# Where the expert tiles, the weight ring and the normalised rows begin in SBUF: from offsets of 96 and 128 bytes to multiples of 512

## The reference

```python
def expert_choice_moe(h, w_router, w_gate_e, w_up_e, w_down_e):
    b, s, _ = h.shape
    cap = EC_CAPACITY * s // N_EXPERTS            # 2 * 512 // 16 = 64 rows for each of 16 experts
    affinity = jax.nn.softmax((h @ w_router).astype(jnp.float32), axis=-1)
    top_aff, idx = lax.top_k(jnp.swapaxes(affinity, 1, 2), cap)
    ...
    xe = h[bidx, idx]
    hid = jax.nn.silu(jnp.einsum('becd,edf->becf', xe, w_gate_e)) * jnp.einsum('becd,edf->becf', xe, w_up_e)
    ye = jnp.einsum('becf,efd->becd', hid, w_down_e)
    return jnp.zeros_like(h).at[bidx, idx].add(ye * top_aff[..., None].astype(ye.dtype))
```

## Time and profile before

| | us |
|---|---|
| median of three executions | 3655.0 |
| the profiled execution | 3652.09 |
| its span, first to last instruction | 3650.3 |

### The profile page before, as it was taken

How to read it: one execution, slowest core, us unless ns; L and a number is a source line. 1 busy time by engine, 2 the same in 40 slices (tenths; PEclk the granted TensorE clock), 3 DMA queues, 4 the chain that set the end, 5 groups by cost and what they waited for, 6 DMA issues and landing times. The chain is left out here.

```text
span 3650.3 us, 41915 instructions
## 1 busy us (share of the span) xinstructions
PE 3420.4 (94%) x17436; PEld 2449.3 (67%) x17436; DVE 1612.1 (44%) x2462; ACT 1138.2 (31%) x1765; POOL 79.8 (2%) x69
## 2 busy tenths in 40 slices
PE   7989998999989989998999988999999999989998
PEld 5767875444437767877444446876788888778887
DVE  3664542111125564552111114434656655466665
ACT  4553321010014454332101003444333344533333
POOL 0000000000000000000000000000000000000000
PEclk9999997999999999998999999999999999999999
DMA  5112254999982212235899992321222322122322
GB/s 168 53 44 79 65 182 189 409 409 409 409 335 95 76 45 67 73 110 209 352 409 409 409 409 100 105 82 47 81 93 94 103 73 78 58 70 93 104 93 70
DMA packets 324091, 616.69 MB, mean 169 GB/s; under 512 B 10864, under 2 KB 210288, under 8 KB 323904
## 3 DMA queue, kind: packets, MB, share of 16 engines
q1 hardware_dynamic: 323904, 614.01, 46.0%
HBM read 609.75 MB, written 4.23 MB: 168 GB/s over the span
## 5 line engine op out<-in xcount | busy, mean ns | idle before, releaser
L421 PE MATMUL bank<-h_hi,w_hi 128*128 128x512 f32 x1864 | 741.3, 398 | 11.1 <-DVE w_lo L207 10.0
L422 PE MATMUL bank<-h_lo,w_hi 128*128 128x512 f32 x1864 | 729.1, 391 | 0.0
L423 PE MATMUL bank<-h_hi,w_lo 128*128 128x512 f32 x1864 | 728.6, 391 | 0.0
L207 DVE TENSOR_TENSOR w_lo<-w_raw,w_hi 128x2048 fp32r<-128x2048 f32 (+1 forms) x209 | 424.1, 2029 | 224.9 <-ACT w_hi L199 224.4
L2063 PE MATMUL bank<-expert_w,gathered 128*64 128x512 f32 x2048 | 455.0, 599 | 30.6 <-DMA expert_w<-in_w_exp_up 27.2
L199 ACT ACTIVATE w_hi<-w_raw 128x2048 fp32r<-128x2048 f32 (+1 forms) x209 | 355.4, 1701 | 242.2 <-PE bank L423 203.8
L421 PEld LDWEIGHTS bank<-h_hi,w_hi 128*128 128x128 f32 x1864 | 351.5, 189 | 101.5 <-issue 16.5
L423 PEld LDWEIGHTS bank<-h_hi,w_lo 128*128 128x128 f32 x1864 | 351.3, 188 | 75.3
L422 PEld LDWEIGHTS bank<-h_lo,w_hi 128*128 128x128 f32 x1864 | 351.7, 189 | 73.0 <-issue 1.9
L2063 PEld LDWEIGHTS bank<-expert_w,gathered 128*64 128x64 f32 x2048 | 153.9, 138 | 314.7 <-issue 314.7
L2063 PE MATMUL bank<-expert_w,hidden_t 128*64 128x512 f32 x1024 | 228.5, 599 | 10.8 <-DMA expert_w<-in_w_exp_down 10.8
(11 more groups left out here) (411 smaller groups left out, 4599.8 us busy)
## 6 DMA issues: line engine op xcount, KB each, us to landing
expert_w<-in_w_exp_gate SPq DMA_DIRECT2D x64, 2048.0 KB, 23.9
expert_w<-in_w_exp_up SPq DMA_DIRECT2D x64, 2048.0 KB, 23.8
expert_w<-in_w_exp_down SPq DMA_DIRECT2D x64, 2048.0 KB, 23.9
w_raw<-in_ffn_w_up SPq DMA_DIRECT2D x44, 1024.0 KB, 5.1
w_raw<-in_w_branch_gate SPq DMA_DIRECT2D x64, 512.0 KB, 4.1
w_raw<-in_w_in SPq DMA_DIRECT2D x22, 1024.0 KB, 5.3
w_raw<-in_ffn_w_down SPq DMA_DIRECT2D x22, 1024.0 KB, 4.9
w_raw<-in_hgrn_w_in SPq DMA_DIRECT2D x16, 1024.0 KB, 5.3
```

Of the source, the lines that this page charges most:

```text
L207: dve.tensor_tensor(self.w_lo[n % 2][:, 0:e], self.raw[n % self.RAW][:, 0:e], self.w_hi[n % 2][:, 0:e].bitcast(F32), ALU.subtract).then_in ...
L421: pe.matmul(out, st[0], mv[0], start=(j == 0), stop=False)
L422: pe.matmul(out, st[0], mv[1], start=False, stop=False)
L423: last = pe.matmul(out, st[1], mv[0], start=False, stop=(j == len(g.steps) - 1))
```

## The change

No instruction is added, taken away or moved. On each of the five engines the order is the same, row by row; only the four scratch instructions of L748 and L749 name `conv_half` in place of `lam_tmp`, and lines of the file after L1834 have other numbers. What changes is where tensors begin:

- `iota64`, `eps`, `rms` and `rstd` (296 bytes of payload) move in front of `h_hi`, and a pad follows them that ends on a multiple of 512.
- `lam_tmp` becomes the first 32 elements of `conv_half`.
- `v.layer_base` is rounded up to a multiple of 512 instead of 32. The room given up and saved is such that it lands 96 bytes lower than before.
- The stage's allocations are moved up to `v.layer_base` by a pad where they start below it.

Worked out from the allocation, the starting byte in each partition is:

| tensors | begin, before | beyond a multiple of 512 | begin, after | beyond | moved by |
|---|---|---|---|---|---|
| `x` | 16512 | 128 | 16512 | 128 | 0 |
| `h_hi`, expert place 2 | 32896 | 128 | 33280 | 0 | +384 |
| `h_lo`, expert place 5 | 49280 | 128 | 49664 | 0 | +384 |
| ring, expert places 6, 7, 8 | 65664, 82048, 98432 | 128 | 66048, 82432, 98816 | 0 | +384 |
| `identity`, `ones`, ... | 114816 | 128 | 115200 | 0 | +384 |
| arena, expert places 0, 1, 3, 4 | 122976, 139360, 155744, 172128 | 96 | 122880, 139264, 155648, 172032 | 0 | -96 |
| `xs` | 188512 | 96 | 188416 | 0 | -96 |
| `merged_hi`, `merged_lo` | 194752, 211136 | 192 | 194656, 211040 | 96 | -96 |
| `y_hi`, `y_lo` of the feed-forward layers (first of four each) | 142144, 150336 | 320 | 142176, 150368 | 352 | +32 |
| `o_hi` (fox; hgrn) | 188416; 191520 | 0; 32 | 188448; 191552 | 32; 64 | +32 |
| `branch_hi`, `branch_lo` | 122976, 139360 | 96 | 122880, 139264 | 0 | -96 |

The sources in HBM do not move. An expert's row of 4096 bytes starts at a multiple of 4096 within its tensor.

```diff
-            order(dve.tensor_tensor(v.lam_tmp[:], lv[:, i * 64:i * 64 + 32], lv[:, i * 64 + 32:i * 64 + 64], ALU.mult))
-            dve.tensor_reduce(v.small[:, i:i + 1], v.lam_tmp[:], AXX, ALU.add).then_inc(*prods.inc())
+            order(dve.tensor_tensor(v.lam_tmp, lv[:, i * 64:i * 64 + 32], lv[:, i * 64 + 32:i * 64 + 64], ALU.mult))
+            dve.tensor_reduce(v.small[:, i:i + 1], v.lam_tmp, AXX, ALU.add).then_inc(*prods.inc())
...
-        assert aligned(nc.sbuf_base) == v.layer_base
+        if v.layer_base > nc.sbuf_base:
+            sb("layer_alignment", [P, (v.layer_base - nc.sbuf_base) // 4])
+        assert nc.sbuf_base == v.layer_base
         sb("expert_arena", [P, 4, 4 * D])
...
         v.x = sb("x", [P, KT, S])
-        v.h_base = aligned(nc.sbuf_base)
+        v.iota64, v.eps = sb("iota64", [P, 64]), sb("eps", [P, 1])
+        v.rms, v.rstd = (sb(n, [P, TB]) for n in ("rms", "rstd"))
+        sb("alignment", [P, -aligned(nc.sbuf_base) % 512 // 4])
+        v.h_base = nc.sbuf_base
         v.h_hi, v.h_lo = sb("h_hi", [P, KT, S], F32R), sb("h_lo", [P, KT, S], F32R)
...
-        v.iota64, v.ones_row, v.eps = sb("iota64", [P, 64]), sb("ones_row", [P, S]), sb("eps", [P, 1])
-        v.rms, v.rstd, v.rms2, v.rstd2, v.unused = (sb(n, [P, TB]) for n in ("rms", "rstd", "rms_second", "rstd_second", "unused"))
+        v.ones_row = sb("ones_row", [P, S])
+        v.rms2, v.rstd2, v.unused = (sb(n, [P, TB]) for n in ("rms_second", "rstd_second", "unused"))
...
-            v.lam_tmp, v.small, v.neg_lam, v.gq, v.gdiff, v.expa = (sb1("lam_tmp", [P, 32]), sb1("small", [P, 8]), sb1("neg_lam", [P, 1]),
+            v.lam_tmp = v.conv_half[:, 0:32]
+            v.small, v.neg_lam, v.gq, v.gdiff, v.expa = (sb1("small", [P, 8]), sb1("neg_lam", [P, 1]),
...
-            v.layer_base = aligned(nc.sbuf_base)
+            v.layer_base = -(-nc.sbuf_base // 512) * 512
```

## The result

| kernel | median of the runs, us | lowest to highest, runs | ratio to before, 95% interval |
|---|---|---|---|
| before | 3654.8 | 3649.96 to 3658.4, 4 | |
| after | 3626.6 | 3623.12 to 3629.08, 4 | 0.9924, 0.9909 to 0.9940 |

The kernel is 28 us faster, 0.76%. The profiled execution took 3626.4 us with a span of 3624.6, which is 25.7 us less than before.

What follows compares the result with a forecast made beforehand. Expert-tile loads were taken to bound the two expert stages, PE's dense products the rest. All terms were 0: 3652.1 us profiled + 0, and 2.9 us more for the median of the runs, gave 3655 us, range 3629 to 3662.

Steps and rivals of the forecast that it cites:

- What bounds the kernel: Expert stages: tile loads at 409 GB/s are 8% slower than PE and set the end; elsewhere PE's dense products.
- The cap of 41.2 us: Both expert stages: all PE waits for tiles, 18.8 + 22.4 us, the most that faster loads could gain.
- The step that failed: Expert tile loads: places at 96 and 128 go at one pace, so aligning to 512 was taken to gain 0 us.
- My bound of plus or minus 6.6 us: Expert tile loads: 0.7% spread between windows, 0.038 us a tile, 3.3 us a stage, up or down.
- The support for that step: Ring loads: `w_in` rows mostly start off 256 in HBM, `hgrn_w_in` rows on it, yet both land in 5.3 us.
- The Trainium skill's rule: DMA transfers: cut at multiples of 256 bytes, and bytes between the boundary below and an odd start cost time too.
- A: Expert tiles: bytes below the start cost time, so aligning saves 2.7% a tile, 24 us, giving 3631 us; chance 10%.
- B: Expert tiles: each 256-byte piece costs the same, 16 for 17; all 41.2 us of waits go, 3614 us; chance 10%.
- C: Matmuls: moving and stationary operands collide at new offsets, 6 us slower for `y`, up to 3705 us with `h`; chance 2%.
- D: Expert places: the change does not do what it says, so no effect; within the 70% for no effect.
- Ring, small tensors: Weight-ring loads and small tensors: 0 us and no new wait; faster ring loads could give at most 4.1 + 3.3 us.
- Operands: Dense products with `y`, `branch`, `merged`, `o`: means of 391 to 400 ns do not follow the offset, so 0 us.

Runs made afterwards that it cites:

- the kernels at 256, 32 and 224: Kernel after with all nine expert places, `h` and the ring 256, 32 or 224 bytes beyond a multiple of 512: 3632.1, 3657.2 and 3657.1 us.

## Why the prediction was wrong

*What bounds the kernel* held. The expert stages gave nearly their 87 tiles times the saving: 5.127 - 4.981 = 0.146 us a tile, x 87 x 2 = 25.4 us, and the stages are 23.5 us shorter, the span 25.7. One reading in it was wrong without harm: nine tiles of lead are 46 us, and at 4.5 us a pair eight pairs would not use them up. PE caught up after about four pairs. A tile lands 23.9 us after its issue, so more than four of the nine places hold tiles that are still on their way, and the lead that counts is the rest.

The cap of 41.2 us was not reached. 19.4 us of it are waits that went; the other 4.1 us show that waits alone are no exact measure of a stage. In the first one PE's waits fell by 7.2 us and the stage by 12.5, while the experts' products with `gathered` went from 229.8 to 224.9 us. From 850 to 1000 us the granted clock was 0.97 on average before, and 1.00, its upper level, after. Before, it fell three times for a few microseconds, each time at a wait of 3.2, 2.8 or 2.7 us for a tile (at 866.9, 928.3 and 989.6 us); but a wait of 3.2 us at 1052.5 us left it at 1.00, and so did waits of 2.6 and 2.8 us in the kernel after. In the second the waits fell by 12.2 us and the stage by 11.0, with the experts' products 2.3 us longer in all. When PE is slower it waits less, and the stage ends where the loads let it. So the clock is seen together with the waits, and that fewer waits kept it up is not shown.

*The step that failed* is "an offset that is a multiple of 128 and one that is only a multiple of 32 go at one pace ... So neither the 32 bytes nor the 64 or 128 count. I extend this to 256 and 512 and take 0 us." The rows were read correctly: places at 96 and at 128 do go at one pace. But two odd starts at one pace can mean that both are free or that both pay the same, and without one aligned tile in the trace the rows can't tell the two apart. Both paid, 4.5 ns for each row of 4096 bytes. The term set at 0 measured 0.146 us a tile. My bound of plus or minus 6.6 us came from the spread between the two odd kinds, which bounds a difference between them and not the distance of both from a third kind.

*The support for that step* was about the other end of the transfer. The source at an odd start is free, which a run now shows; I had let that speak for the destination.

*The Trainium skill's rule* ("DMA: Bandwidth & Descriptors", "How a descriptor splits into AXI transactions") speaks of bytes below the start that are "fetched but unused and still cost beats", and its words are about reading; for writes it states no cost. On the side that reads the runs show no cost, 421 GB/s at a start 128 bytes off. Taken for the side that writes, as I took it, it has the direction right against my zero and not the size: 409 GB/s at 32, at 96 and 128, and at 224 alike.

*The rivals.* A gave 2.7%, 24 us, 3631 us, 420 GB/s and waits near 7 and 10 us; measured were 2.8% of a tile's time, 25.7 us of the span, 3626.6 us, 421 GB/s and waits of 11.6 and 10.2. Its nearness is luck: it owes this to 96 and 128 being near the one value at which bytes below the start cost as much as the flat price, and I gave it 10% where its objection, no difference between 96 and 128, told only against its mechanism. B (434 GB/s from its 4.83 us a tile, no waits) was about twice too large. C did not come: `h` stays at 391 ns. D was excluded by the rate.

*Ring, small tensors* at 0 held: the landings of the earlier trace rows fell by 0.1 to 0.4 us, ACT's waits of the earlier trace rows for two of these loads by 1.9 us together, PE waited for none of them, and `h` did not change.

*Operands* at 0 held for the sum, within 2 us by their groups, but the statement that the means do not follow the offset did not. `y` reads 394 three times at 192 bytes from the ring's offset, 399, 395 and 393 at 352 bytes, and 389 at 0. The same three numbers 399, 395 and 393 stand in the kernels at 256, 32 and 224, where `y` begins elsewhere but at the same distance, so the start alone does not count. The distance may, but it is not the whole: at one and the same distance the three products read 399, 395 and 393.

## What to carry to other kernels

Where a stretch is bound by loads into SBUF, put the destination's rows at multiples of 256 bytes, and make the rows long: here these gave 409 to 421 and 421 to 430 GB/s, and only a stretch whose end the loads set turns that into time. When a trace holds only misaligned cases, their equal pace is no evidence that alignment is free; a bound drawn from them does not hold for the aligned case, and the forecast should be kept wide or leave the sign to a rule that speaks of it. When a base is moved for one tensor, look at what else stands relative to it, as `y` against the ring does.

## What the runs showed of the hardware

- A load's row that begins off a multiple of 256 bytes in SBUF costs 4.4 to 4.5 ns more on its DMA engine (worked out from 421 against 409 GB/s, and 408 against 387), the same for 32, 96, 128 and 224, and the same for rows of 2048 and 4096 bytes. That holds when all tiles are odd; among aligned tiles it is less (417 and 418 GB/s with four and five of nine places aligned). Other offsets, such as 64 or 192, were not tried on the tiles, and why it is half of what 256 bytes take stays open.
- An odd start in HBM, by 128 bytes, costs nothing where the places in SBUF are aligned: 421 GB/s and 3625.9 us.
- A row costs about 4.9 ns beyond its bytes, so 2048, 4096 and 16,384 bytes give 408, 421 and 430 GB/s when aligned.
- The mean of the 128x512 products with `y` is 389 ns when both operands begin at the same offset from a multiple of 512, 394 when their offsets are 192 bytes apart, and 393 to 399 at 352 bytes. No mechanism is shown. The edit that brings `y` to 389 ns, together with the other tensors that it moves, is worth 5 to 9 us in this kernel. The fastest version that computes the reference is the kernel after with that repaired, at 3620 to 3621 us. The long rows with the gathered rows put in the same order as them were not tried.
